# A two-layer decoder trunk on one core: the SBUF layout turned round, overlaid regions lowest

## The chip, the cores and the metric

One Trainium2 chip, one of its cores. The metric is the device time of one execution in microseconds. The median of three runs of the kernel before is 2397.23 us (2395.22 to 2398.16).

## The reference

Two layers over 512 tokens of width 1024, everything float32:

```python
for l in range(DEPTH):
    h = h + 0.5 * swiglu(rmsnorm(h, ffn1_norm[l]), ffn1_w_in[l], ffn1_w_out[l])
    u = rmsnorm(h, mix_norm[l])
    q_a, c_kv, iq, ik, iw, z_pool, q_c, gate_pre = jnp.split(u @ w_in[l], split_pts, axis=-1)
    y_a = dsa_attention(q_a, c_kv, iq, ik, iw, w_uk[l], w_uv[l], rel_bias)   # top-128 of the causal keys
    y_b = pool_mixer(z_pool, w_pool[l], pool_scale[l])
    y_c = mem_attention(q_c, rmsnorm(mem, mem_norm[l]), w_mem_kv[l])
    g = jax.nn.sigmoid(gate_pre).reshape(B, S, N_BRANCH, D)
    merged = (g[:, :, 0] * (y_a @ w_branch_a[l]) + g[:, :, 1] * (y_b @ w_branch_b[l])
              + g[:, :, 2] * (y_c @ w_branch_c[l]))
    h = h + merged @ w_out[l]
    h = h + 0.5 * swiglu(rmsnorm(h, ffn2_norm[l]), ffn2_w_in[l], ffn2_w_out[l])
return rmsnorm(h, final_norm)
```

A SwiGLU block has a hidden width of 2816.

## The kernel before, in words

The activations lie transposed, features on the 128 partitions and the 512 tokens in the row, eight tiles of 128 x 512 for a width of 1024. A row of such a tile is 512 floats, 2048 bytes. Every large product is made with split operands: a float32 value is kept as a high part in fp32r and a low part (what the rounding left), and three matmuls of 128x128 by 128x512 stand for one exact tile product: high by high (line 517), low weight by high activation (518), high weight by low activation (519). This is the function `exact`. TensorE loads the 128x128 weight tile and streams the 512 columns of the activation tile past it; the streamed operand is called the moving one here, the loaded one the stationary one.

- **Weights.** SP sends each unit of weights (up to 128 x 1024) from HBM into one of four slots of `raw`. GpSimd (POOL) splits it into `wH` and `wL` (lines 468 and 471), two slots each. TensorE uses a unit, then frees the slot. The order of the units is written out by hand, the same on all engines, and counted by semaphores.
- **FFN** (twice a layer): the hidden tiles come from `u0H`/`u0L` (24 matmuls a unit of 1024 columns), in two halves of 12 and 10 tiles, and go to `hidH`/`hidL`; VectorE (DVE) and ScalarE (ACT) apply norm, sigmoid, gate and split. The down projection streams `hidH`/`hidL` (18 or 15 matmuls a unit).
- **Mixer**: the memory keys and values (lines 605 to 607, 617 to 619, 256 columns; in the first three the normed memory in `yH`/`yL` is the moving operand, in the last three the weights are), the projection `W_in` from `u1H`/`u1L` in slots into which the attention's small matmuls are set by a plan, the gated branches from `yH`/`yL` (a part in the gate slots, `W_branch_a` after them), and `W_out`, again from `u1H`/`u1L`.
- **Start**: in `block.scalar`, lines 851 to 858, a table of T5 biases is written from the tile `q` to HBM (`bias_rows`) and read back spread over the partitions. ACT's first norm step stands behind the first of these two.

**Memory.** `sb(name, shape)` takes the next free piece of each partition's SBUF, in the order of the calls, rounded up to a multiple of 32 bytes; leaving an `ExitStack` gives its pieces back, so that the next stack overlays them. First come the tiles that live through the whole kernel (`h`, `u1H`, `u1L`, `raw`, `wH`, `wL`, tables, scratch), and above them four stacks on one another: `ffn` (`u0H`, `u0L`, `hidH`, `hidL`, `mem`), `mix` (`yH`, `yL`, `gate_a`, `q`, `probs` and others), `index` and `late`. `exact` is:

```python
for i, (t, k) in enumerate(tiles):
    a, b = wH[:, w, t * P:(t + 1) * P], wL[:, w, t * P:(t + 1) * P]
    pe.matmul(dst, a, hi[:, k, :], start=first and i == 0, stop=False)
    pe.matmul(dst, b, hi[:, k, :], start=False, stop=False)
    mm = pe.matmul(dst, a, lo[:, k, :], start=False, stop=last and i == len(tiles) - 1)
```

Of the kernel before, what the change touches and what calls it, by code (L numbers as in the profile page):

```python
# [22 lines left out]
F32R = mybir.dt.float32r  # L23
# [4 lines left out]
P = 128  # L28
D = 1024
T = 512  # L30
L = 2
M = 256
KD = D // P
QB = T // P
H = 8
HD = 64
R = 128
IH = 8
# [14 lines left out]
RAW_SLOTS, SPLIT_SLOTS, BANKS = 4, 2, 4  # L53
# [15 lines left out]
W_POOL, W_UK, W_UV, N_PAR = 35, 163, 675, 1187  # L69

K_ID, K_ONE, K_CAUSAL, K_COUNT, K_GAIN, N_CONST = 0, 128, 256, 384, 416, 424

N_SCORES = 3 * IH
NBIAS = 384


def attention_steps():
# [91 lines left out]
def bucket_of(n):  # L169

    exact = BUCKETS // 2
    nf = np.maximum(n, 1).astype(np.float32)
    large = exact + (np.log(nf / np.float32(exact)) / np.float32(math.log(MAXDIST / exact))
                     * np.float32(BUCKETS - exact)).astype(np.int32)
    return np.where(n < exact, n, np.minimum(large, BUCKETS - 1))


def constants():
# [6 lines left out]
    for g, w in enumerate(WINDOWS):  # L185
        rows = slice(64 * (g % 2), 64 * (g % 2) + 64)
        first = 1.0 / np.minimum(np.arange(1, WMAX + 1), w)
        c[rows, K_COUNT + WMAX * (g // 2):K_COUNT + WMAX * (g // 2) + WMAX] = first
    buckets = bucket_of(np.maximum(255 - np.arange(NBIAS), 0))
    hot = (np.arange(BUCKETS)[:, None] == buckets[None, :]).astype(np.float32)  # L190
# [3 lines left out]
def trunk(nc, xT, memT, wA, wB0, wB1, wM, wR, par, const, hot, rel, out, bias_rows):  # L194
    ctx = ExitStack()
    with ctx:
        def sb(name, shape, dt=F32, scope=ctx):
            return scope.enter_context(nc.sbuf_tensor(name, shape, dt))
# [2 lines left out]
            return ctx.enter_context(nc.semaphore(name))  # L201


        h = sb("h", [P, KD, T])
        u1H, u1L = sb("u1H", [P, KD, T], F32R), sb("u1L", [P, KD, T], F32R)
        raw = sb("raw", [P, RAW_SLOTS, 8 * P])
        wH = sb("wH", [P, SPLIT_SLOTS, 8 * P], F32R)
        wL = sb("wL", [P, SPLIT_SLOTS, 8 * P], F32R)
        near_bias = sb("near_bias", [P, H, 2 * P])
        far_bias = sb("far_bias", [P, H])  # L210
        cst = sb("cst", [P, N_CONST])
        pr = sb("pr", [P, N_PAR])
        rms = sb("rms", [P, T])
        mem_rms = sb("mem_rms", [P, M])
        ssq = sb("ssq", [P, T])
        sq = sb("sq", [P, T])
        ta = sb("ta", [P, T])
        tb = sb("tb", [P, T])
        sg = sb("sg", [P, 2, T])
        iw = sb("iw", [P, QB, IH])  # L220
        norm = sb("norm", [P, 3, QB])
        top8 = sb("top8", [P, 8])
        nmax = sb("nmax", [P, 4, 2])
        rsum = sb("rsum", [P, 4, 2])
        rinv = sb("rinv", [P, 4, 2])

        with ExitStack() as ffn:
            u0H, u0L = sb("u0H", [P, KD, T], F32R, ffn), sb("u0L", [P, KD, T], F32R, ffn)
            hidH = sb("hidH", [P, HALF[0], T], F32R, ffn)
# [29 lines left out]
        with ExitStack() as late:  # L259
            sb("hole0", [P, 2, KD, T], F32, late)  # L260
            sb("hole1", [P, KD, T], F32, late)
            part = sb("part", [P, KD, T], F32, late)
            gate_bc = sb("gate_bc", [P, 2, T], F32, late)
        mem_hi = yH[:, 0:4, :].rearrange("p a (b m) -> p (a b) m", m=M)
        mem_lo = yL[:, 0:4, :].rearrange("p a (b m) -> p (a b) m", m=M)
        c_tok = ssq[:, :].rearrange("p (b r) -> p b r", r=R)
# [11 lines left out]
        rel_sb = q[0:BUCKETS, 1, 0:H]  # L278
        bias_table = q[0:H, 2, 0:NBIAS]

# [125 lines left out]
        def _(sp):  # L406
            sp.dma_start(cst[:, :], const).then_inc(const_loaded, 16)

            sp.dma_start(q[0:BUCKETS, 0, 0:NBIAS], hot).then_inc(rel_loaded, 16)
            sp.dma_start(q[0:BUCKETS, 1, 0:H], rel).then_inc(rel_loaded, 16)  # L410
# [86 lines left out]
        def _(pe):  # L497
# [34 lines left out]
            def spread(diag, n, cols=T):  # L532
# [6 lines left out]
            pe.wait_ge(rel_loaded, 32)  # L539
            pe.matmul(sbank[0][0:H, 0:NBIAS], rel_sb, q[0:BUCKETS, 0, 0:NBIAS], start=True, stop=True  # L540
                      ).then_inc(bias_full, 1)
# [284 lines left out]
        def _(act):  # L826
# [13 lines left out]
            for k in range(KD):  # L840
# [4 lines left out]
                if k:  # L845
# [4 lines left out]
            act.wait_ge(bias_full, 1)  # L850
            act.activation(bias_table, sbank[0][0:H, 0:NBIAS], ACT.Copy).then_inc(bias_copied, 1)
            act.wait_ge(bias_copied, 1)

            act.dma_start(bias_rows, bass.AP(tensor=bias_table.tensor, offset=bias_table.offset,
                                             ap=[bias_table.ap[0], [0, P], [1, NBIAS]])).then_inc(bias_stored, 16)
            act.wait_ge(bias_stored, 16)
# [666 lines left out]
```

## Time and profile before

| | before |
|---|---|
| median of three runs | 2397.23 us |
| the profiled execution, its own time | 2396.16 us |
| its span, first to last instruction | 2394.3 us |
| TensorE matmul (PE) busy | 2312.5 us, 97% |
| GpSimd (POOL) busy | 1389.6 us, 58% |
| VectorE (DVE) busy | 1249.8 us, 52% |
| ScalarE (ACT) busy | 560.3 us, 23% |
| granted TensorE clock, mean | 0.989 |

The profile is of one execution. Its span leaves out 1.9 us that the time of the same execution holds. The durations of matmuls overlap, since they are pipelined and their ends are modelled: what one costs is read from the distance between two starts.

### The profile page before, as it was taken

What the parts mean: (1) busy time and instruction counts of PE and PEld (TensorE: products, weight loads), DVE (VectorE), ACT (ScalarE), POOL (GpSimd) and SP (SyncE); (2) the same over time, 40 slices, a digit from 0 to 9 for tenths busy, and PEclk for the clock granted to TensorE, in tenths of its full rate; (3) what the DMA queues carried; (4) which work ended last, traced back from release to release, by engine and by line L of the source; (5) the groups of instructions that cost most, each with busy time, mean ns of one, the idle gap of its engine ahead of it and who ended that gap; (6) DMA issues with size and microseconds to landing.
All of it is one profiled execution on the core that took longest, in us unless ns stands there. A gap on an engine that the chain in (4) does not pass through costs nothing.

```text
span 2394.3 us, 31804 instructions
## 1 busy us (share of the span) xinstructions
PE 2312.5 (97%) x10328; PEld 1846.1 (77%) x10328; DVE 1249.8 (52%) x1756; ACT 560.3 (23%) x1038; POOL 1389.6 (58%) x868
## 2 busy tenths in 40 slices
PE   3999999999999999999999999999999999999997
PEld 2788888777877788888778888877777778888875
DVE  2453355478865755225454524636787566440453
ACT  1211112243455221001121101214334532110111
POOL 2566666634434666666666666664344366666663
PEclk8999999999999999999999999999999999999998
DMA  5233223311121322232232332232121122223222
GB/s 136 90 116 95 97 87 98 101 58 66 58 67 49 112 91 89 88 104 85 81 107 96 110 103 91 80 110 80 54 64 61 53 97 89 97 79 105 96 76 73
DMA packets 66482, 208.74 MB, mean 87 GB/s; under 512 B 7352, under 2 KB 9560, under 8 KB 66136
## 3 DMA queue, kind: packets, MB, share of 16 engines
q1 hardware_dynamic: 63600, 202.84, 25.7%
q10 hardware_dynamic: 2792, 4.72, 0.9%
q8 instruction: 54, 0.88, 0.2%
q14 instruction: 36, 0.29, 0.0%
HBM read 203.86 MB, written 3.67 MB: 87 GB/s over the span
## 4 chain that ended last, share of the span: by engine, by line
PE 89%; DVE 7%; DMA 2%; issue 1%; ACT 1%; DVEq 0%; ACTq 0%
PE bank L517 27%; PE bank L519 27%; PE bank L518 27%; DMA bias_rows<-q 1%; PE obank L737 1%; PE sbank L689 1%; PE tbank L710 1%; DVE u1L L1429 1%; DVE picks L1229 1%; DVE picks L1252 1%; DVE tb L1443 1%; PE sbank L684 1%; PE obank L724 1%; DVE top L1227 1%; PE sbank L671 1%
## 5 line engine op out<-in xcount | busy, mean ns | idle before, releaser
L468 POOL TENSOR_SCALAR wH<-raw 128x1024 fp32r<-128x1024 f32 (+3 forms) x432 | 438.2, 1014 | 944.6 <-PE bank L519 926.8
L471 POOL TENSOR_TENSOR wL<-raw,wH 128x1024 fp32r<-128x1024 f32 (+3 forms) x432 | 951.5, 2202 | 36.0
L517 PE MATMUL bank<-u0H,wH 128*128 128x512 f32 x1408 | 563.3, 400 | 6.9 <-POOL wL L471 4.1
L518 PE MATMUL bank<-u0H,wL 128*128 128x512 f32 x1408 | 559.7, 398 | 0.0
L519 PE MATMUL bank<-u0L,wH 128*128 128x512 f32 x1408 | 559.7, 397 | 0.0
L517 PEld LDWEIGHTS bank<-u0H,wH 128*128 128x128 f32 x1408 | 266.1, 189 | 76.5 <-issue 8.5
L518 PEld LDWEIGHTS bank<-u0H,wL 128*128 128x128 f32 x1408 | 266.4, 189 | 65.3 <-issue 1.2
L519 PEld LDWEIGHTS bank<-u0L,wH 128*128 128x128 f32 x1408 | 266.2, 189 | 65.0
L517 PE MATMUL bank<-u1H,wH 128*128 128x512 f32 x704 | 295.7, 420 | 7.5 <-DVE u1L L1429 3.1
L517 PE MATMUL bank<-hidH,wH 128*128 128x512 f32 x704 | 279.6, 397 | 0.7 <-DVE hidL L1132 0.7
L518 PE MATMUL bank<-hidH,wL 128*128 128x512 f32 x704 | 279.1, 396 | 0.0
L519 PE MATMUL bank<-hidL,wH 128*128 128x512 f32 x704 | 279.0, 396 | 0.0
L519 PE MATMUL bank<-u1L,wH 128*128 128x512 f32 x704 | 275.9, 392 | 0.0
L518 PE MATMUL bank<-u1H,wL 128*128 128x512 f32 x704 | 274.9, 391 | 0.0
L1123 DVE TENSOR_TENSOR tb<-bank,rms 128x512 f32<-128x512 f32 x88 | 60.8, 691 | 356.4 <-PE bank L519 356.4
L1129 DVE TENSOR_TENSOR sg<-ta,tb 128x512 f32<-128x512 f32 x88 | 232.4, 2641 | 3.0
L869 ACT ACTIVATE hidH<-sg 128x512 f32 x88 | 55.6, 632 | 698.6 <-DVE sg L1129 698.6
L517 PEld LDWEIGHTS bank<-u1H,wH 128*128 128x128 f32 x704 | 132.3, 188 | 51.9 <-issue 20.0
L517 PEld LDWEIGHTS bank<-hidH,wH 128*128 128x128 f32 x704 | 132.6, 188 | 33.8 <-DVE hidL L1132 1.5
L519 PEld LDWEIGHTS bank<-hidL,wH 128*128 128x128 f32 x704 | 132.6, 188 | 32.3
L518 PEld LDWEIGHTS bank<-hidH,wL 128*128 128x128 f32 x704 | 132.6, 188 | 32.2
L519 PEld LDWEIGHTS bank<-u1L,wH 128*128 128x128 f32 x704 | 132.1, 188 | 29.6
(175 smaller groups left out, 2411.0 us busy)
## 6 DMA issues: line engine op xcount, KB each, us to landing
raw<-in_wA SPq DMA_DIRECT2D x176, 512.0 KB, 3.3
raw<-in_wM SPq DMA_DIRECT2D x96, 512.0 KB, 3.3
raw<-in_wB SPq DMA_DIRECT2D x64, 384.0 KB, 3.0
raw<-in_wB SPq DMA_DIRECT2D x64, 320.0 KB, 2.9
raw<-in_wR SPq DMA_DIRECT2D x32, 256.0 KB, 2.6
h<-in_xT ACTq DMA_DIRECT2D x4, 512.0 KB, 6.8
mem<-in_memT SPq DMA_DIRECT2D x2, 1024.0 KB, 6.8
outT<-gate_a SPq DMA_DIRECT2D x4, 512.0 KB, 2.7
```

What stands on the lines that cost most here:

```text
L468: pool.tensor_scalar(wH[:, w, 0:cols], raw[:, slot, 0:cols], 1.0, 0.0, ALU.mult, ALU.add).then_inc(rounded, 1)
L471: pool.tensor_tensor(wL[:, w, 0:cols], raw[:, slot, 0:cols], wH[:, w, 0:cols].bitcast(F32), ALU.subtract).then_inc(split_done, 1)
L517: pe.matmul(dst, a, hi[:, k, :], start=first and i == 0, stop=False)
L518: pe.matmul(dst, b, hi[:, k, :], start=False, stop=False)
L519: mm = pe.matmul(dst, a, lo[:, k, :], start=False, stop=last and i == len(tiles) - 1)
L671: mm = pe.matmul(dst[:, j * M:(j + 1) * M], qc[rows, j, a * P:(a + 1) * P], kc[rows, j, :], start=True, stop=True)
L684: mm = pe.matmul(dst[:, j * P:(j + 1) * P], pr[rows, W_UK + P * j:W_UK + P * (j + 1)], q[rows, j, a * P:(a + 1) * P], start=True, stop=True)
L689: mm = pe.matmul(dst[:, 0:width], qlat[:, b, :], ckv[:, 0:width], start=True, stop=True)
L710: mm = pe.transpose(tbank[:, kb * P:(kb + 1) * P], probs[:, m % 3, kb * P:(kb + 1) * P], ident)
L869: act.activation(hidH[:, bass.ds(j * 2 + i, 1), :].rearrange("p a t -> p (a t)"), sg[:, 1, :], ACT.Copy).then_inc(hidden_high, 1)
L1123: dve.tensor_tensor(tb[:, :], bank[2 * i + 1][:, :], rms[:, :], ALU.mult).then_inc(evacuated, 1)
L1129: dve.tensor_tensor(sg[:, 1, :], ta[:, :], tb[:, :], ALU.mult).then_inc(gated, 1)
```

## The change

The four overlaid stacks are opened first, from the lowest free address on, and after them one piece `overlays` of 24,704 floats (98,816 bytes) takes their place for good, so that the tiles of the whole kernel come above. Nothing else is changed: every engine has the same instructions on the same tiles in the same order, three lines further down in the file.

```diff
+OVERLAYS = 24704
...
+        with ExitStack() as ffn:
+            u0H, u0L = sb("u0H", [P, KD, T], F32R, ffn), sb("u0L", [P, KD, T], F32R, ffn)
+            hidH = sb("hidH", [P, HALF[0], T], F32R, ffn)
+            hidL = sb("hidL", [P, HALF[0], T], F32R, ffn)
+            mem = sb("mem", [P, KD, M], F32, ffn)
+        with ExitStack() as mix:
+            yH, yL = sb("yH", [P, KD, T], F32R, mix), sb("yL", [P, KD, T], F32R, mix)
...
+        with ExitStack() as late:
...
+            gate_bc = sb("gate_bc", [P, 2, T], F32, late)
+        sb("overlays", [P, OVERLAYS])
 
         h = sb("h", [P, KD, T])
         u1H, u1L = sb("u1H", [P, KD, T], F32R), sb("u1L", [P, KD, T], F32R)
...
         rinv = sb("rinv", [P, 4, 2])
-
-        with ExitStack() as ffn:
-            u0H, u0L = sb("u0H", [P, KD, T], F32R, ffn), sb("u0L", [P, KD, T], F32R, ffn)
...
```

The start of each tile in a partition, in bytes, as the built programs have it. All overlaid tiles move down by 112,288 and all others up by 98,816:

| tile | start before | mod 64 | start after | mod 64 |
|---|---|---|---|---|
| h | 16,512 | 0 | 115,328 | 0 |
| u1H, u1L | 32,896; 49,280 | 0 | 131,712; 148,096 | 0 |
| raw (4 slots) | 65,664 | 0 | 164,480 | 0 |
| wH, wL | 82,048; 90,240 | 0 | 180,864; 189,056 | 0 |
| near_bias | 98,432 | 0 | 197,248 | 0 |
| cst | 106,656 | 32 | 205,472 | 32 |
| pr | 108,352 | 0 | 207,168 | 0 |
| rms, ssq, sq, ta, tb, sg | 113,120 to 124,384 | 32 | 211,936 to 223,200 | 32 |
| u0H, yH | 128,800 | 32 | 16,512 | 0 |
| u0L, yL | 145,184 | 32 | 32,896 | 0 |
| hidH, gate_a | 161,568 | 32 | 49,280 | 0 |
| hidL | 186,144 | 32 | 73,856 | 0 |
| q | 198,432 | 32 | 86,144 | 0 |
| mem, probs | 210,720 | 32 | 98,432 | 0 |

A tile's rows of 512 floats follow one another at steps of 2048 bytes, so each has the remainder of its tile.

## Rows read from the trace of the kernel before

**Rows 1.** The page: span, TensorE's share, its granted clock, and the chain by engine.
```profile
span 2394.3 us, 31804 instructions
...
PE 2312.5 (97%) x10328; PEld 1846.1 (77%) x10328; DVE 1249.8 (52%) x1756; ACT 560.3 (23%) x1038; POOL 1389.6 (58%) x868
...
PEclk8999999999999999999999999999999999999998
...
PE 89%; DVE 7%; DMA 2%; issue 1%; ACT 1%; DVEq 0%; ACTq 0%
```
**Rows 2.** Timeline of PE, last W_out unit into FFN: start, length (us), line, tiles.
```profile
831.97 0.39 PE L517 MATMUL bank<-u1H,wH 128*128 128x512 f32 x1
...
837.41 0.40 PE L517 MATMUL bank<-u0H,wH 128*128 128x512 f32 x1
...
838.11 0.39 PE L517 MATMUL bank<-u0H,wH 128*128 128x512 f32 x1
...
842.80 0.40 PE L519 MATMUL bank<-u0L,wH 128*128 128x512 f32 x1
```
**Rows 3.** Timeline of PE, among the gate slots of layer 0.
```profile
683.17 0.39 PE L517 MATMUL bank<-u1H,wH 128*128 128x512 f32 x1
...
684.98 0.39 PE L519 MATMUL bank<-u1L,wH 128*128 128x512 f32 x1
...
700.28 0.39 PE L518 MATMUL bank<-yH,wL 128*128 128x512 f32 x1
...
702.61 0.39 PE L519 MATMUL bank<-yL,wH 128*128 128x512 f32 x1
```
**Rows 4.** Line 518 by tile: count, ns min/median/max, first and last start, forms.
```profile
L518 PE MATMUL bank<-u0H,wL x1408: 392/397/628, 13.7 to 2317.5; 128*128 128x512 f32 x176
L518 PEld LDWEIGHTS bank<-hidH,wL x704: 187/188/192, 186.8 to 2374.1; 128*128 128x128 f32 x176
L518 PE MATMUL bank<-hidH,wL x704: 392/397/400, 187.1 to 2374.4; 128*128 128x512 f32 x176
...
L518 PE MATMUL bank<-u1H,wL x704: 387/389/402, 443.3 to 2000.9; 128*128 128x512 f32 x176
...
L518 PE MATMUL bank<-yH,wL x128: 388/394/400, 616.5 to 1953.7; 128*128 128x512 f32 x128
```
**Rows 5.** Timeline of PE, the 256-column products of the memory projection.
```profile
424.80 0.28 PE L607 MATMUL bank<-yL,wH 128*128 128x256 f32 x1
...
427.26 0.28 PE L607 MATMUL bank<-yL,wH 128*128 128x256 f32 x1
...
439.32 0.28 PE L619 MATMUL bank<-wH,yL 128*128 128x256 f32 x1
...
441.83 0.28 PE L619 MATMUL bank<-wH,yL 128*128 128x256 f32 x1
```
**Rows 6.** Stretches: length, busy us and counts by engine, PEclk, DMA share, GB/s.
```profile
0.00:59.00 59.00, 21.23 (x70) 13.98 (x70) 17.32 (x18) 11.71 (x18) 14.94 (x12) 0.83 0.54 138
...
764.00:792.00 28.00, 26.64 (x112) 20.56 (x111) 22.16 (x23) 11.23 (x18) 21.52 (x19) 1.00 0.35 113
```
**Rows 7.** Timeline of ACT at the start: the store and load of the biases.
```profile
24.39 1.28 ACTq L854 DMA_DIRECT2D bias_rows<-q  x1
59.21 0.39 ACTq L858 DMA_DIRECT2D near_bias<-bias_rows  x1
```
**Rows 8.** Waits of PE: us in total, times, longest.
```profile
PE obank L535 <- DVE tb L1086: 31.6, 2, 29.1
```
**Rows 9.** Groups by form, PE: a short attention product (busy us, mean ns).
```profile
L684 PE MATMUL sbank<-q,pr 64*128 64x128 f32 x128 | 18.5, 285 | 0.0
```
**Rows 10.** Groups by form, POOL: splitting a 640-column unit (busy us, mean ns).
```profile
L471 POOL TENSOR_TENSOR wL<-raw,wH 128x640 fp32r<-128x640 f32 x64 | 103.2, 1612 | 5.3
...
L468 POOL TENSOR_SCALAR wH<-raw 128x640 fp32r<-128x640 f32 x64 | 48.8, 763 | 80.7 <-PE bank L519 80.7
```

More of the change, by code:

```diff
@@ L201, in sem @@
             return ctx.enter_context(nc.semaphore(name))
[L204 to L225, printed above, removed]
         with ExitStack() as ffn:
@@ L263, in trunk @@
             gate_bc = sb("gate_bc", [P, 2, T], F32, late)
+        sb("overlays", [P, OVERLAYS])
+        h = sb("h", [P, KD, T])
+        u1H, u1L = sb("u1H", [P, KD, T], F32R), sb("u1L", [P, KD, T], F32R)
+        raw = sb("raw", [P, RAW_SLOTS, 8 * P])
+        wH = sb("wH", [P, SPLIT_SLOTS, 8 * P], F32R)
+        wL = sb("wL", [P, SPLIT_SLOTS, 8 * P], F32R)
+        near_bias = sb("near_bias", [P, H, 2 * P])
+        far_bias = sb("far_bias", [P, H])
+        cst = sb("cst", [P, N_CONST])
+        pr = sb("pr", [P, N_PAR])
+        rms = sb("rms", [P, T])
+        mem_rms = sb("mem_rms", [P, M])
+        ssq = sb("ssq", [P, T])
+        sq = sb("sq", [P, T])
+        ta = sb("ta", [P, T])
+        tb = sb("tb", [P, T])
+        sg = sb("sg", [P, 2, T])
+        iw = sb("iw", [P, QB, IH])
+        norm = sb("norm", [P, 3, QB])
+        top8 = sb("top8", [P, 8])
+        nmax = sb("nmax", [P, 4, 2])
+        rsum = sb("rsum", [P, 4, 2])
+        rinv = sb("rinv", [P, 4, 2])
         mem_hi = yH[:, 0:4, :].rearrange("p a (b m) -> p (a b) m", m=M)
```

## The prediction

> **What bounds the kernel now.** The page comes first: TensorE has a matmul in flight for 97% of the 2394.3 us, its clock is granted in full in nearly every slice, and the chain that ends last is 89% TensorE [rows 1]. So the time is the number of matmuls times the distance between their starts, and I read distances. The change adds, removes and reorders no instruction; it can act only through addresses. The question for the trace is therefore whether a matmul's price depends on where its operands lie, and for that I compared like products on different tiles.
>
> The border between `W_out` and the second FFN is the cleanest place [rows 2]. From 831.97 to 837.41 TensorE starts 24 matmuls that stream `u1H`/`u1L`: 5.44 us, **226.7 ns each**. From 837.41 to 842.80 it starts 23 more that stream `u0H`/`u0L`: 5.39 us, **234.3 ns each**. Shape, types, weight buffers and clock are the same and nothing lies between. The reader is to see a step at the moment when the moving tile changes. In the gate slots it happens inside one stage, in both directions [rows 3]: 8 steps on `u1` take 1.81 us (226 ns), 10 steps on `y` 2.33 us (233 ns). And it holds everywhere: over all uses the median modelled length is 397 ns for `u0`, 397 for `hid`, 394 for `y` and 389 for `u1`, with minima of 392, 392, 388 and 387 [rows 4].
>
> What do the dear tiles have in common? In the table of starts, `u0`, `hid` and `y` begin 32 bytes past a multiple of 64, `u1` on one; the stationary `wH`/`wL` are on one for all. It isn't merely that the dear ones lie above 131,072 bytes: the first tile of `u0H` spans 128,800 to 130,848, and its three matmuls (the third streams `u0L`) take 838.11 - 837.41 = 0.70 us, 233 ns each, like the rest [rows 2]. As an estimate from the rows: were a 2048-byte row read in pieces of 64 bytes, a start on a multiple would need 32 pieces and a start 32 off 33, and 226.7 x 33/32 = 233.8, beside 234.3 measured. One row speaks against so simple a picture: among the 256-column products, 21 steps with `y` moving take 2.46 us (117.1 ns) and 21 with the weights moving and `y` stationary 2.51 us (119.5 ns) [rows 5]. There one operand is 32 off in both forms, so they say nothing of two aligned operands, but they show no toll on the moving side alone. After the change every moving tile of line 517 to 519 and every weight tile is on a multiple of 64, which is the state of `u1` today.
>
> **The change part by part.**
>
> *FFN products.* 1408 on each of three lines for `u0` and 704 on each for `hid`, as line 518 shows [rows 4]: 3 x 2112 = 6336. At the start some are covered: up to 59 us 70 matmuls have run, 10 of them for biases and norm, so 60 of the FFN [rows 6], and then TensorE waits up to 29.1 us for the norm's `tb` [rows 8], which waits for ACT behind the bias store. These 60 save nothing. The toll: 234.3 - 226.7 = 7.6 at the border [rows 2], 233 - 226 = 7 in the gate slots [rows 3]; I take 7.1 ns, between the two and equal to 1/33 of 234.3. 6276 x 7.1 = **44.6 us**. Bounds are the differences of medians [rows 4]: `y` less `u1`, 5 ns, gives 31.4; `u0` less `u1`, 8 ns, gives 50.2. Does TensorE stay the bound? The tightest feeder is the 640-column unit: 15 matmuls fall from 3.51 to 3.41 us, and POOL needs 0.763 + 1.612 = 2.38 us for its split [rows 10]. It keeps 1 us.
>
> *Branch products on `y`.* 3 x 128 = 384. Half of them stand in the gate slots, where TensorE is the chain: 192 x 7.1 = **1.4 us**. The other half are `W_branch_a`, where DVE is busy 22.2 of 28 us with the merging and TensorE 26.6 [rows 6]; what they save is waited for at the first merged tile of `W_out`. I cost this half at 0, with 1.4 us as the upper bound; the cover is DVE's chain, and without it the 1.4 us come too.
>
> *Small products of the attention* (128 on `q` [rows 9], as many on `ckv`, fewer on `kc` and `ik_stack`) stream short rows, some 370 in all. At most 7.1 ns each, 2.6 us; at least 0, since their neighbours' waits may take it. I take **1.0 us**. The 256-column products I cost at 0.
>
> *`u1` products* (2112) keep their remainder and their weights' remainder: 0. *DVE, ACT, POOL:* `raw`, `wH`, `wL`, `rms`, `ta`, `tb`, `sg` all move by the same 98,816 bytes, a multiple of 64: 0, under TensorE's cover.
>
> *The bias store.* From issue at 24.39 to the next instruction at 59.21, 34.8 us pass [rows 7], and nearly all of it is on the path. It reads eight partitions of `q`, which move from 32 to 128 bytes past a multiple of 256. I know no row that prices this; I take 0, with -1 and +2 us as bounds. The Trainium skill (DMA: Bandwidth & Descriptors, How a descriptor splits into AXI transactions) has a transaction begin on a multiple of 256 bytes: an estimate by it is 49 beats for a packet before and 52 after, 6% more, or about 2 us longer; with it the sum would be 2 us worse. No run here shows it yet.
>
> *What comes back.* Between the hidden products and the down projection the last gate and split of DVE take as long as before while TensorE arrives sooner, so some of these eight borders lose a little: **-0.5 us**.
>
> Sum: 44.6 + 1.4 + 1.0 - 0.5 = 46.5 us. The profiled execution took 2396.16 us, 1.07 under the median of 2397.23; taken from that median, 2350.7 us. **Forecast 2350.5 us**, 1.95% faster. Within its own case it lies between 2343 (8 ns, and something from `y` and the short products: 2350.7 - 5.6 - 2) and 2366 (5 ns: 2350.7 + 13.2, and the DMA 2 longer).
>
> **The rivals.**
>
> *B: no difference, 2397 us.* The step belongs to something other than the start: what DVE and ACT do beside, or which tile they are writing. For it: FFN, `hid` and `y` differ from `u1` in more than address, and the 256-column rows show no toll [rows 5]. Against: inside one stage the price goes up for `y` and back for `u1` [rows 3], at full clock and with the same neighbours. The Trainium skill (SBUF — State Buffer, Specifications) gives 16-byte cachelines with a penalty for each new line; both remainders are multiples of 16, so by that rule a row crosses equally many lines and the change is worth nothing. Chance 10%.
>
> *C: height, not remainder, 2365 us.* The toll begins somewhere between 65,664 (the end of `u1L`) and 128,800. Then `u0`, `hid`, `y` come free, 46.5 us, and `u1`, now from 131,712 on, pays: 2112 x 7.1 = 15.0. 2397.2 - 46.5 + 15.0 = 2365.7. If `hidL` above 73,856 kept its toll, 704 x 7.1 = 5 more. For it: the trace can't exclude it. Against: no threshold lies at a natural place, 131,072 being excluded by the first tile of `u0H`. Chance 6%.
>
> *D: slower.* TensorE reads two streams at once, weights and moving columns. Before, no moving tile above 131,072 bytes ever met weights that lay there too, since `wH`/`wL` were at 82,048 to 98,432. Afterwards the 2112 products on `u1` do. Should the two reads get in each other's way in one half, the products of `W_in` and `W_out` grow. A load takes 188 ns [rows 4], hidden under the stream; bounds are 0 and 188 ns a product. The point from which the kernel gets slower is 46.5 us / 2112 = 22 ns. At a quarter of a load, 47 ns, it is 2350.7 + 99 = 2450 us. Against: no tile shows such a toll in the present layout. Chance 3%.
>
> **How the numbers follow.** Forecast 80%, B 10%, C 6%, D 3%, and 1% for what I don't see. The forecast's own range holds some 95% of its case, 0.76, and half of C lies inside it, 0.03: together about 0.80, so the range is 2343 to 2366. A measurement of this kernel can tell about 0.2% (4.8 us) from no change. Faster is the forecast and C, 0.86; same is B, 0.10; slower is D and half of the rest, 0.04.
>
> **What would show it.** In the profile afterwards the step at the border from `u1` to `u0` is gone and both go at 227 ns; line 518 has a median of 389 ns for all four tiles; POOL waits some 45 us less for TensorE, while the busy time of DVE, ACT and POOL stays. C would show `u0` at 227 and `u1` at 234; B the same step as now; D a `u1` distance above 250 ns. The forecast is wrong if `u0` isn't below 230 ns, or if it is and the time falls by less than 35 us: then a wait has taken the gain, and I would look at the bias store and at `W_out`'s first tiles.

## The result and the profile after

The changed kernel takes **2346.84 us** (median of four runs, 2344.18 to 2348.62), the kernel before 2397.55 us in the four runs beside and before it. The ratio is 0.9787, with a 95% interval of 0.9775 to 0.9799: 2.1% faster, 50.7 us. The forecast was 2350.5 in a range of 2343 to 2366. The profiled execution took 2346.86 us with a span of 2345.0 (before: 2396.16 and 2394.3).

The page after, in the lines that answer to [rows 1]:

```profile
span 2345.0 us, 31804 instructions
...
PE 2263.2 (97%) x10328; PEld 1839.8 (78%) x10328; DVE 1250.0 (53%) x1756; ACT 560.1 (24%) x1038; POOL 1406.7 (60%) x868
...
PEclk8999999999999999999999999999999999999998
...
PE 87%; DVE 8%; DMA 2%; ACT 1%; issue 1%; DVEq 0%; POOL 0%; ACTq 0%; POOLq 0%
```

The instruction counts are the same to the last one, DVE and ACT are busy as long as before (1250.0 and 560.1 us against 1249.8 and 560.3), and the span and the busy time of TensorE have both fallen by 49 us. POOL is busy for 17.1 us more (1406.7 against 1389.6), which the prediction didn't expect. It is the border between `W_out` and the second FFN that shows where the gain came from, as in [rows 2] (timeline of PE: start, length in us):

```profile
821.62 0.39 PE L520 MATMUL bank<-u1H,wH 128*128 128x512 f32 x1
...
827.06 0.39 PE L520 MATMUL bank<-u0H,wH 128*128 128x512 f32 x1
...
832.27 0.39 PE L522 MATMUL bank<-u0L,wH 128*128 128x512 f32 x1
```

24 starts from 821.62 to 827.06 are 226.7 ns apart, as before; the 23 that follow, on `u0`, take 5.21 us, 226.5 ns. The step of 7.6 ns is gone. Line 518 is line 521 now, and its median lengths have come together, where [rows 4] had 397, 397 and 394 beside 389 (count, ns min/median/max):

```profile
L521 PE MATMUL bank<-u0H,wL x1408: 387/389/628, 14.4 to 2270.3; 128*128 128x512 f32 x176
...
L521 PE MATMUL bank<-hidH,wL x704: 387/389/397, 182.7 to 2325.4; 128*128 128x512 f32 x176
...
L521 PE MATMUL bank<-yH,wL x128: 387/389/402, 606.7 to 1916.5; 128*128 128x512 f32 x128
```

By stage, from stretches of the two traces that begin and end with the same instructions (length, then busy us and counts of PE, PEld, DVE, ACT, POOL). Before: the first down projection, then the mixer of layer 0 without `W_out`, then the first hidden half of the second FFN:

```profile
186.80:254.60 67.80, 67.80 (x293) 54.55 (x291) 16.84 (x20) 5.15 (x10) 44.42 (x32) 1.00 0.31 98
...
443.00:791.70 348.70, 342.73 (x1667) 269.73 (x1667) 242.02 (x473) 152.42 (x330) 159.77 (x105) 1.00 0.20 67
...
837.40:974.10 136.70, 136.70 (x587) 109.76 (x586) 71.11 (x70) 25.00 (x33) 89.14 (x48) 1.00 0.26 90
```

The same after:

```profile
182.50:248.20 65.70, 65.70 (x294) 54.45 (x292) 16.50 (x21) 5.15 (x10) 44.39 (x33) 1.00 0.33 103
...
433.20:781.30 348.10, 341.98 (x1666) 269.65 (x1666) 241.66 (x474) 152.33 (x330) 159.94 (x105) 1.00 0.21 67
...
827.10:959.50 132.40, 132.40 (x588) 109.41 (x587) 71.00 (x70) 24.98 (x33) 90.81 (x48) 1.00 0.28 92
```

The FFN stretches lose 3.1% of their length, the mixer 0.6 us of 348.7. Read from the exact first start of each stage, the FFN stretches (with the start, the memory projection and the tail) differ by 47.8 us in all, the two mixers with `W_out` by 1.5.

The memory projection is one stage where the two traces differ for another reason. Its two uses before, then its two uses after:

```profile
424.50:443.00 18.50, 15.33 (x107) 14.34 (x107) 8.48 (x18) 2.73 (x4) 14.35 (x9) 0.91 0.35 113
1586.80:1607.00 20.20, 16.98 (x107) 16.00 (x107) 8.36 (x18) 2.74 (x4) 14.48 (x9) 0.83 0.32 104
```

```profile
413.10:433.20 20.10, 17.05 (x107) 15.96 (x107) 8.30 (x18) 2.73 (x4) 14.41 (x9) 0.83 0.32 104
1553.60:1570.70 17.10, 14.03 (x106) 13.00 (x106) 8.56 (x18) 2.73 (x4) 14.41 (x9) 1.00 0.36 123
```

The column before the DMA share is TensorE's granted clock. Where it is below 1, a part of these products starts at 213 ns distances in place of 112 to 120: that part ran at the lower of the clock's two levels (1.2 in place of 2.4 GHz), after a pause of TensorE that leads up to it (busy 1.22 of 3.00 us from 415 to 418 us in the trace after). The first use became 1.6 us longer and the second 3.0 us shorter. In the eleven kernels of this document each use takes about 17.1, 18.5 or 20.1 us, and the toll doesn't order them: the four kernels with the FFN at 226.7 ns have 20.1 and 17.1 three times and 18.6 and 18.6 once. So these 1.4 us net are not the step that was forecast, and whether the change brought them isn't shown.

### The profile page after: what moved, and what is told of

Read it like the earlier page. It is cut to its first block, busy times and chain, and to the rows that moved or that the text cites. A ratio compares the mean times of both kernels' runs of the same rounds, so it can differ in the third digit from the quotient of the medians.

```text
span 2345.0 us, 31804 instructions
## 1 busy us (share of the span) xinstructions
PE 2263.2 (97%) x10328; PEld 1839.8 (78%) x10328; DVE 1250.0 (53%) x1756; ACT 560.1 (24%) x1038; POOL 1406.7 (60%) x868
## 4 chain that ended last, share of the span: by engine, by line
PE 87%; DVE 8%; DMA 2%; ACT 1%; issue 1%; DVEq 0%; POOL 0%; ACTq 0%; POOLq 0%
PE bank L520 27%; PE bank L522 26%; PE bank L521 26%; PE obank L740 1%; DMA bias_rows<-q 1%; PE sbank L692 1%; PE tbank L713 1%; DVE u1L L1432 1%; DVE tb L1446 1%; DVE picks L1232 1%; DVE picks L1255 1%; PE sbank L687 1%; PE obank L727 1%; DVE top L1230 1%; PE sbank L674 1%
## 5 line engine op out<-in xcount | busy, mean ns | idle before, releaser
L471 POOL TENSOR_SCALAR wH<-raw 128x1024 fp32r<-128x1024 f32 (+3 forms) x432 | 454.6, 1052 | 878.7 <-PE bank L522 862.0
L520 PE MATMUL bank<-u0H,wH 128*128 128x512 f32 x1408 | 553.2, 393 | 7.7 <-POOL wL L474 4.5
L522 PE MATMUL bank<-u0L,wH 128*128 128x512 f32 x1408 | 549.6, 390 | 0.0
L521 PE MATMUL bank<-u0H,wL 128*128 128x512 f32 x1408 | 549.4, 390 | 0.0
L522 PE MATMUL bank<-hidL,wH 128*128 128x512 f32 x704 | 274.0, 389 | 0.0
L521 PE MATMUL bank<-hidH,wL 128*128 128x512 f32 x704 | 273.9, 389 | 0.0
L1132 DVE TENSOR_TENSOR sg<-ta,tb 128x512 f32<-128x512 f32 x88 | 232.2, 2638 | 3.0
L521 PEld LDWEIGHTS bank<-u1H,wL 128*128 128x128 f32 x704 | 132.6, 188 | 28.2 <-issue 3.4
```

The source lines that it names most:

```text
L471: pool.tensor_scalar(wH[:, w, 0:cols], raw[:, slot, 0:cols], 1.0, 0.0, ALU.mult, ALU.add).then_inc(rounded, 1)
L1132: dve.tensor_tensor(sg[:, 1, :], ta[:, :], tb[:, :], ALU.mult).then_inc(gated, 1)
```

## The experiments

The twelve runs (numbered 1 to 12) either move tiles and do nothing else, or measure the products by themselves. "48 starts" counts the distances from the first row shown to the second. "d" is the start of the moving tile less the start of its weight buffer, modulo 256 bytes; it is 160 for `u0`, `hid` and `y` in the kernel before, 0 in the changed one, and 0 for `u1` in both. This quantity wasn't in the prediction; it came out of the first four runs.

**1. 32 bytes ahead of the overlaid tiles, in the kernel before.**

```diff
+        sb("pad", [P, 8])
         with ExitStack() as ffn:
```

> The kernel before with 32 bytes put between the whole kernel's tiles and the overlaid ones: u0, hid and y stay high (from 128,832) but now begin on a multiple of 64. Theory R (the remainder of the moving tile by 64 sets the price, 227 or 234 ns): all four tiles at 227 ns, 2347 us, the same as the changed kernel. Theory H (height: tiles high in SBUF are dear): u0 and hid stay at 234 ns, 2397 us. Theory M (mismatch: dear when the remainders of moving and stationary tile differ): as R, 2347 us.

Measured: 2389.48 us, ratio to before 0.9973 (0.9963 to 0.9983). The moving tiles lay on multiples of 64, and yet 48 starts on `u0` took 11.20 us, 233.3 ns each (timeline of PE):

```profile
859.82 0.39 PE L518 MATMUL bank<-u0H,wH 128*128 128x512 f32 x1
...
871.02 0.39 PE L518 MATMUL bank<-u0H,wH 128*128 128x512 f32 x1
```

Theory R, the one of my prediction, fell here: on a multiple of 64 the product still costs 6.6 ns too much. Theory M as it is written, with remainders by 64, fell with it, since both operands were on multiples of 64; it can live on only with a longer period.

**2. The changed kernel with its overlaid tiles 32 bytes higher.**

```diff
+        sb("pad", [P, 8])
         with ExitStack() as ffn:
...
-        sb("overlays", [P, OVERLAYS])
+        sb("overlays", [P, OVERLAYS + 8])
```

> The changed kernel with every overlaid tile 32 bytes higher and all others 64 bytes higher: u0, hid and y lie low but 32 past a multiple of 64; u1 and the weights stay on multiples. R and M: u0, hid, y at 234 ns, u1 at 227, 2397 us (2394 to 2399). H: all at 227 ns, 2347 us.

Measured: 2390.29 us, 0.9975 of before (0.9963 to 0.9986). 48 starts take 11.20 us, 233.3 ns:

```profile
859.71 0.40 PE L521 MATMUL bank<-u0H,wH 128*128 128x512 f32 x1
...
870.91 0.40 PE L521 MATMUL bank<-u0H,wH 128*128 128x512 f32 x1
```

Lying low is worth nothing: theory H fell. All but about 6 us of the change can be lost by shifting the low tiles by 32 bytes. The time is 4 us under the range expected by R and M, since the toll was 6.6 ns here and 7.6 before.

**3. Everything 32 bytes higher.** As run 2, with `OVERLAYS` left as it is.

> The changed kernel with every tile 32 bytes higher, so that moving and stationary tiles are all 32 past a multiple of 64. R: every product pays, u1 too: 234 ns throughout and 2397 + 2112 x 7.1 = 2412 us. M: the remainders agree, 227 ns throughout, 2347 us. H: 2347 us.

Measured: 2348.9 us, 0.9804 of before (0.9789 to 0.9818), with every tile of line 517 to 519 and every weight tile 32 past a multiple of 64. 48 starts take 10.88 us, 226.7 ns:

```profile
859.71 0.39 PE L521 MATMUL bank<-u0H,wH 128*128 128x512 f32 x1
...
870.59 0.39 PE L521 MATMUL bank<-u0H,wH 128*128 128x512 f32 x1
```

So no tile's own remainder explains the toll. What the good runs share is the difference between the moving tile and the weights.

**4. The weight buffers alone 32 bytes higher, in the changed kernel.**

```diff
+        sb("pad", [P, 8])
         wH = sb("wH", [P, SPLIT_SLOTS, 8 * P], F32R)
         wL = sb("wL", [P, SPLIT_SLOTS, 8 * P], F32R)
+        sb("pad_after", [P, 8])
```

> The changed kernel with wH and wL alone 32 bytes higher (the tiles behind them 64): moving tiles on multiples of 64, weights 32 past. R and H: 227 ns throughout, 2347 us. M: 234 ns throughout, 2412 us. If a weight load that starts off a multiple costs TensorE something of its own, the load of 188 ns gets longer while the start distance of 227 ns stays.

Measured: 2394.72 us, the same as before (0.9995, 0.9985 to 1.0004). No moving tile was touched, and they all became dear, `u1` with them: 48 starts on `u0` in 11.20 us and 24 on `u1` in 5.60, 233.3 ns each:

```profile
821.93 0.40 PE L522 MATMUL bank<-u1H,wH 128*128 128x512 f32 x1
...
827.53 0.40 PE L522 MATMUL bank<-u1H,wH 128*128 128x512 f32 x1
...
860.07 0.40 PE L522 MATMUL bank<-u0H,wH 128*128 128x512 f32 x1
...
871.27 0.40 PE L522 MATMUL bank<-u0H,wH 128*128 128x512 f32 x1
```

A mismatch between the two operands is what is left, theory M with another period. Run 1 narrows it: there both tiles were on multiples of 64 and the product was still dear, so the period is above 64 bytes. M's own number, 2412 us, was 17 too high. The toll on `u0` and `hid` was 6.6 ns, where its sum keeps the 7.6 of before, and `u1` didn't pay in full: the two mixers with `W_out` take 797.3 us against 787.3 in the changed kernel, 10.0 us for 2112 products on `u1` and 384 on `y`, some 4 ns each. The loads themselves are no longer than before, 188 ns in the median in every kernel.

**5. The four FFN tiles at odd places**, in the changed kernel: each is a view into a tile 16 floats longer, 4, 12, 1 and 2 floats in for `u0H`, `u0L`, `hidH`, `hidL`.

```diff
+            def off(name, n, words):
+                whole = sb(name, [P, n * T + 16], F32R, ffn)
+                return whole[:, words:words + n * T].rearrange("p (a t) -> p a t", t=T)
```

> The changed kernel with the four FFN tiles at other remainders by 64: u0H 16, u0L 48, hidH 4, hidL 8 bytes; u1 and y stay at 0. Theory R in pieces of 64 bytes (a row that starts anywhere inside a piece touches 33 of them): 234 ns for all three products of u0 and of hid, as with 32, and 2394 to 2399 us. Theory S (16-byte lines: only a start inside a line costs): u0 at 227, hid at 234 or above, 2347 + 2112 x 7.1 = 2362 us. A toll that grows with the remainder would set u0L (48) above u0H (16) and hid lowest.

Measured: 2407.35 us in one run, 9 us above the before of that hour (2398.14). d is 16 and 112 for `u0H` and `u0L`, 132 and 200 for `hidH` and `hidL`. On `u0` 48 starts take 11.31 us (235.6 ns), on `hid` 11.52 us (240.0 ns):

```profile
859.92 0.40 PE L523 MATMUL bank<-u0H,wH 128*128 128x512 f32 x1
...
871.23 0.40 PE L523 MATMUL bank<-u0H,wH 128*128 128x512 f32 x1
...
1009.60 0.41 PE L523 MATMUL bank<-hidH,wH 128*128 128x512 f32 x1
...
1021.12 0.41 PE L523 MATMUL bank<-hidH,wH 128*128 128x512 f32 x1
```

Both theories fell, R with 234 ns for all four tiles and S with 227 ns for `u0`. It is no matter of yes or no: the price is graded, and the layout before wasn't the worst.

**6. The products by themselves.** A program in which nothing but TensorE runs after the loading.

> A program by itself: 192 products to warm up, then blocks of 96 products each, with nothing running beside on any other engine: streamed tile 0, 32, 16, 48 or 4 bytes past a multiple of 64 with weights on a multiple, then 0 and 32 with weights 32 past; rows of 512, 384 and 256 columns. It computes none of the reference. R with one piece more for a row: 7 ns more for every start off 0, at each of the three lengths, unless the 188 ns load limits. A rate theory (each piece of a row off a multiple costs a little): 7 ns at 512 columns, 5 at 384, 3.5 at 256. If the toll comes only from other engines' traffic: no difference between blocks.

The blocks don't divide by the moving tile's remainder, and the 7 ns that R wanted for every start off 0, at each length, isn't there: the order of the prices is another at each length. The tiles' starts made d 192, 160, 80, 240, 4, 96 and 64 in the order of the blocks; d = 0 wasn't among them. For example, d = 4 and then d = 96 and 64 (line by tile: count, ns min/median/max, first and last start):

```profile
L55 PE MATMUL bank<-mfour,wzero x96: 390/399/406, 149.3 to 171.8; 128*128 128x512 f32 x96
L55 PE MATMUL bank<-mzero,whalf x96: 391/394/400, 172.0 to 194.2; 128*128 128x512 f32 x96
L55 PE MATMUL bank<-mhalf,whalf x96: 387/392/397, 194.4 to 216.2; 128*128 128x512 f32 x96
```

With 95 steps in each they go, by the exact starts, at 236.5, 233.3 and 229.0 ns. d = 160 (82.21 to 104.47 us) gave 234.3 ns, exactly what the kernel before shows at 160. Two things follow: the toll needs no other engine, since none runs; and it is set by the two operands of TensorE itself.

**7. The remaining tiles on multiples of 64**, a pad of 8 floats behind each tile whose length leaves the next one 32 past.

> The changed kernel with the remaining tiles that begin 32 past a multiple (cst, rms, mem_rms, ssq, sq, ta, tb, sg and the small ones) moved onto multiples of 64 by pads. R: only the attention's short products on sg and cst and the nine norm products on tb and ssq could gain; their start distance is about 110 ns, set by something other than the stream, so 2347 us within 2 us. If ACT, DVE or POOL had a toll too, their durations on ta, tb, sg would fall (DVE 691 ns, ACT 633 ns) but not the time by more than 3 us.

Measured: 2346.58 us, 0.9782 of before (0.9769 to 0.9796), no different from the changed kernel; DVE's and ACT's durations stand. `u0` goes at 226.7 ns (10.88 us for 48 starts). Scratch and tables needn't be touched.

**8. The kernel before with 96 bytes in place of 32.** d becomes 0, and the overlays stay on top.

```diff
+        sb("pad", [P, 24])
         with ExitStack() as ffn:
```

> The kernel before with 96 bytes, in place of 32, put between the whole kernel's tiles and the overlaid ones. u0, hid and y stay high (from 128,896). Counted from the weight buffers, the moving tiles now begin a multiple of 128 bytes away, as u1 does in every fast run so far. Theory D (the distance between moving tile and weight tile, by a multiple of 128, sets the price): all four tiles at 227 ns and 2347 us, like the changed kernel, with the overlays still on top. Theory R (moving tile alone, by 64) has fallen; a height theory gives 2397 us; a theory of 512 (u0 is now 256 past one) gives 233 ns and 2390 us.

Measured: **2346.81 us**, 0.9791 of before (0.9778 to 0.9805). 48 starts take 10.88 us, 226.7 ns:

```profile
859.75 0.39 PE L520 MATMUL bank<-u0L,wH 128*128 128x512 f32 x1
...
870.63 0.39 PE L520 MATMUL bank<-u0L,wH 128*128 128x512 f32 x1
```

That is the whole of the change's gain from one pad of 96 bytes, without turning anything round. It also limits the period: `u0` was 256 past a multiple of 512 from the weights, so the period divides 256. Theory D with 128 bytes says the same here; runs 9 and 12 tell them apart.

**9. The price by distance**, products by themselves.

> A program by itself, computing none of the reference: 96 products a block, streamed tile a multiple of 512 bytes from the weights plus 0, 4, 8, 16, 48 and then 32, 64 up to 480 bytes, rows of 512, then 384, then 256 columns. Theory D128: at 512 columns 227 ns at plus 0, 128, 256 and 384, and 229 to 237 ns elsewhere. D256: 227 at 0 and 256 alone. D512: at 0 alone. The two earlier points taken over: plus 192 at 233.3, plus 32 at 234. If any distance gives less than 227 ns, there is a better layout than the changed one. At 256 columns, 117 to 123 ns with another pattern, since the load of the next weights takes another place in the stream.

Blocks of 96 products, 95 steps, at 512 columns (the tile's name tells its distance from the weights beyond a multiple of 512):

```profile
L54 PE MATMUL bank<-plus000b,w x96: 389/389/389, 44.8 to 66.4; 128*128 128x512 f32 x96
L54 PE MATMUL bank<-plus004b,w x96: 395/398/401, 66.6 to 89.1; 128*128 128x512 f32 x96
...
L54 PE MATMUL bank<-plus064b,w x96: 387/392/394, 178.4 to 200.2; 128*128 128x512 f32 x96
...
L54 PE MATMUL bank<-plus128b,w x96: 392/394/398, 222.8 to 245.0; 128*128 128x512 f32 x96
...
L54 PE MATMUL bank<-plus160b,w x96: 388/397/400, 245.2 to 267.5; 128*128 128x512 f32 x96
...
L54 PE MATMUL bank<-plus256b,w x96: 389/389/395, 312.5 to 334.0; 128*128 128x512 f32 x96
...
L54 PE MATMUL bank<-plus384b,w x96: 392/395/398, 401.0 to 423.2; 128*128 128x512 f32 x96
```

From the exact starts the distances are 226.7 ns at 0, 236.6 at 4, 233.3 at 32, 228.9 at 64, 233.4 at 128, 234.2 at 160, 233.2 at 192 and 224, 226.7 at 256, 229.0 at 320, 233.4 at 384. From 256 on the list repeats to within 0.2 ns at the eight places 0 to 224 in steps of 32: at 512 columns **the period is 256 bytes**, D128 and D512 fell. At other lengths the list is another one. At 256 columns (busy us, mean ns) d = 0 is among the dear places and 64 and 192 are cheap in this program:

```profile
L54 PE MATMUL bank<-plus000b,w 128*128 128x256 f32 x96 | 11.7, 283 | 0.0
...
L54 PE MATMUL bank<-plus192b,w 128*128 128x256 f32 x96 | 11.1, 276 | 0.0
L54 PE MATMUL bank<-plus064b,w 128*128 128x256 f32 x96 | 11.0, 276 | 0.0
```

By starts these are 119.8, 113.7 and 113.4 ns; at 384 columns everything lies between 173.3 and 176.6. At 256 columns the difference modulo 256 doesn't settle the price: 320 gave 117.8 ns where 64 gave 113.4, and run 6 had 117.8 at both 64 and 192. At 384 columns run 6 reached 179.9, at d = 240.

**10. The same in steps of 4 bytes.**

> A program by itself, computing none of the reference: 64 blocks of 72 products, 512 columns, streamed tile a multiple of 512 bytes from the weights plus 0, 4, 8 up to 252 bytes. Theory D256 with the changed kernel at the best place: 226.7 ns at plus 0 and no lower value anywhere. Rival: some distance between the multiples of 16 tried so far is cheaper, which would give a layout better than the changed one (each ns is 8.8 us of the kernel, 8832 products of 512 columns). Points taken over: 0, 4, 8, 16, 32, 48, 64 at 226.7, 236.6, 233.2, 231.7, 233.3, 230.0, 228.9.

Blocks of 72 products, 71 steps:

```profile
L54 PE MATMUL bank<-plus000b,w x72: 389/389/390, 67.1 to 83.1; 128*128 128x512 f32 x72
...
L54 PE MATMUL bank<-plus020b,w x72: 399/404/405, 150.4 to 167.4; 128*128 128x512 f32 x72
...
L54 PE MATMUL bank<-plus028b,w x72: 387/387/391, 184.4 to 200.5; 128*128 128x512 f32 x72
...
L54 PE MATMUL bank<-plus240b,w x72: 388/388/389, 1073.5 to 1089.6; 128*128 128x512 f32 x72
```

The 64 places run from 226.7 to 239.9 ns; 226.7 or 226.9 is reached at 0, 28, 60, 156, 236, 240 and 252, and nowhere is it less. So within this family of layouts the changed kernel's 512-column products are at the floor. Two places came out unlike in two programs (48: 230.0 and 233.2; 240: 233.3 in run 6, 226.7 here), with the same d: it doesn't settle everything. What else does is open.

**11 and 12. Two middle places in the kernel**: pads of 160 and of 224 bytes in the kernel before, d = 64 and 128 (`[P, 40]` and `[P, 56]` in the diff of run 8).

> The kernel before with 160 bytes between the whole kernel's tiles and the overlaid ones: u0, hid and y begin 64 bytes past a multiple of 256 from the weights. Theory D256 with the micro program's price list: 229 ns, between the two states so far, and 2347 + 6276 x 2.2 = 2361 us. A yes-or-no theory of 64 bytes (on a multiple: 227): 2347 us. A yes-or-no theory of 128: 233 to 234 ns, 2390 us.

> The same with 224 bytes: u0, hid and y begin 128 bytes past a multiple of 256 from the weights. D256: 233.4 ns and 2347 + 6276 x 6.7 = 2389 us. D128 (any multiple of 128 is cheap): 227 ns and 2347 us.

Measured: 2362.86 us, 0.9853 of before (0.9837 to 0.9869), and 2382.14 us, 0.9937 (0.9921 to 0.9954). 48 starts take 10.99 us (229.0 ns) with the pad of 160:

```profile
859.83 0.39 PE L520 MATMUL bank<-u0L,wH 128*128 128x512 f32 x1
...
870.82 0.39 PE L520 MATMUL bank<-u0L,wH 128*128 128x512 f32 x1
```

and 11.16 us (232.5 ns) with the pad of 224:

```profile
860.02 0.39 PE L520 MATMUL bank<-u0L,wH 128*128 128x512 f32 x1
...
871.18 0.40 PE L520 MATMUL bank<-u0L,wH 128*128 128x512 f32 x1
```

The price list of run 9 carries over to the kernel within 0.1 ns at 64 and within 0.9 ns at 128 (233.4 there), where the 2389 us expected are 7 too many. Both yes-or-no theories fell, and so did D128. Put together, with 226.7 ns as the floor and 6276 products on `u0` and `hid`:

| kernel | d | start distance, ns | 2346.8 + 6276 x excess, us | measured, us |
|---|---|---|---|---|
| before, pad 96 | 0 | 226.7 | 2346.8 | 2346.8 |
| changed, all 32 up | 0 | 226.7 | 2346.8 | 2348.9 |
| before, pad 160 | 64 | 229.0 | 2361.2 | 2362.9 |
| before, pad 224 | 128 | 232.5 | 2383.2 | 2382.1 |
| before, pad 32 | 192 | 233.3 | 2388.2 | 2389.5 |
| changed, overlays 32 up | 224 | 233.3 | 2388.2 | 2390.3 |
| before | 160 | 234.3 | 2394.5 | 2397.6 |

The sum misses the measured times by -1.1 to 3.1 us. Of that the bias store accounts for 0, 0.9 or 1.7 us, by its own list below: 1.7 in "before", "all 32 up" and "overlays 32 up", 0.9 with the pads of 32 and 160, 0 with those of 96 and 224. What is then left is -1.1 to 1.4 us, for `y`, the short products, the memory projection's clock and the scatter of the medians; it isn't divided further. Two kernels aren't in the table. With the odd places of run 5, means of 235.4 ns on `u0` and 238.3 on `hid` over the whole trace give 2346.8 + 36.2 + 24.5 = 2407.5 us, and 2407.35 were measured. With the weights moved (run 4), 41.4 for the FFN and the 10.0 us of the mixers give 2398.2 us: the profiled execution took 2397.8, but the median of ten is 2394.7, so this one is 3.5 us too high.

## Why the prediction was right, and where its reason was wrong

**The bound and the place** were right. The time is the number of matmuls times the distance of their starts; those on `u0`, `hid` and `y` changed to the distance of `u1`; nothing took more than some 2 us of the gain on the way. What would prove the forecast wrong (`u0` not below 230 ns, or less than 35 us) didn't come. Of the other signs, the medians of line 518 are all 389 ns, as said; POOL waits 65 us less for TensorE, not 45, and its busy time didn't stay.

**The step that failed** is "What do the dear tiles have in common?". I read from the table of starts that the moving tile's own remainder by 64 decided, and even had an estimate that agreed, 226.7 x 33/32 = 233.8. Runs 1, 3 and 4 each break it: 233.3 ns on a multiple of 64, 226.7 ns 32 off one, 233.3 ns after moving only the weights. What decides is the distance between moving tile and weight tile, with a period of 256 bytes. In the two layouts the prediction compared, both rules say the same, because `wH` and `wL` stood on a multiple of 64 in both and `u0` happened to fall 128 bytes into 256 like them; the rows of one kernel that I used could not tell them apart. So it was luck that the reason I had gave the right place for the tiles: a layout turned round with another sum of sizes could have put them on multiples of 64 and won only some 6 us, as run 1 did. The estimate 226.7 x 33/32 agreed by luck too. The 256-column rows [rows 5] were the warning: they showed no toll on the moving side alone, and I named them and went on. Run 9 shows that such products have another price list, and the rows fit it: `y` moving had d = 160 (117.1 ns there, 117.4 in run 9), the weights moving had 96 (119.5 and 120.0).

**The terms.**

- *FFN products*, forecast 44.6 us: the toll was 234.3 - 226.8 = 7.5 ns (means of all start distances under 260 ns, before and after), not 7.1, so 47.1 us; the start distances themselves, added up, fell by 47.2. The measured step of 7.6 ns at the border was the better reading; I had leaned on the gate slots and on the 1/33 of a wrong picture. These 0.4 ns on 6276 products are most of what the sum, 46.5 us, was short of.
- *`y` and short products*, forecast 1.4 and 1.0: the two mixers together with `W_out` are only 1.5 us shorter (0.6 and 1.0 for the mixers, 0 for `W_out`). Of these `W_branch_a`, costed at 0 for its cover by DVE, gave 0.7 (0.2 and 0.5), so the cover was not whole; the gate slots and the short products gave 0.9 of the 2.4 that I had for them. Why so little is open.
- *The memory projection*, forecast 0: 1.4 us shorter in all, and that is the granted clock of the rows above. The layout made a part of it dearer: its 256-column products with `y` moving went from 117.4 to 117.8 ns to 119.3 to 119.4 at full clock, as run 9's list has it for 160 and 0.
- *The bias store*, forecast 0 with -1 and +2: from issue to the next instruction 33.1 us in place of 34.8 [rows 7]:

```profile
25.13 1.28 ACTq L857 DMA_DIRECT2D bias_rows<-q  x1
58.27 0.39 ACTq L861 DMA_DIRECT2D near_bias<-bias_rows  x1
```

  It is 1.7 us shorter and began 0.7 later. PE's wait for the norm behind it fell by 1.4 (29.5 to 28.0 us between the two starts). The source's remainder by 128 goes with it in all eleven kernels: 33.1 to 33.2 us at 0 (six kernels), 34.0 at 64 (pads of 32 and 160), 34.8 at 32 (before, overlays 32 up, all 32 up). The Trainium skill (DMA: Bandwidth & Descriptors, How a descriptor splits into AXI transactions) gave an estimate of 6% more for this step, since 128 past a multiple of 256 makes a longer tail than 32 past one. The trace shows 5% less for the whole store, and no difference between a source 0 past a multiple of 256 (pad of 224, 33.1 us) and one 128 past (the changed kernel, 33.1), where the rule has 48 and 52 beats. So the rule doesn't price this store; the time of the read alone isn't shown.
- *What comes back*, forecast -0.5 at the borders of the hidden products: 0.1 there (TensorE's waits for `hidL` are 0.8 us against 0.7). But the FFN stages as a whole, with the bias store's 1.4, lost 0.5 us outside the plain steps, so 1.9 came back elsewhere: 0.4 at the first weight unit, 0.5 in three products at the lower clock level after the first norm (starts 427 ns apart, where before they were at 333, 232 and 237), the rest in small pieces.
- *Feeders:* POOL kept up, and waits less for TensorE: 862 us against 927 before its first split operation. TensorE's waits for its weights at line 517 (now 520) grew from 6.8 to 7.9 us. The first split of a 1024-column unit takes 1196 ns in place of 1153, which makes 11.7 of the 17.1 us that POOL is busier. All four kernels at 226.7 ns have it (1405.8 to 1407.0 us busy), the one at 229.0 has most of it (1404.4), those at 232.5 ns and more little or none (1386.1 to 1394.4); what lengthens it is open.

The sum of what was measured is 47.2 (steps of the FFN) - 0.5 (the rest of the FFN stages, the bias store in it) + 1.5 (mixers) + 1.4 (memory projection, by the clock) - 0.4 (the first product comes later) = 49.2 us; the spans of the two profiled executions differ by 49.3. The medians differ by 50.7; the 1.4 between them is within the scatter of the executions.

**The rivals.** B, no difference, is excluded by the result and by the programs of runs 6, 9 and 10, in which nothing runs beside. C, height, is excluded by runs 2 and 8: low tiles can be dear and high ones cheap. D spoke of TensorE's two reads getting in each other's way, by the half of SBUF they lie in. The halves play no part (`u1` above 131,072 bytes with the weights there too goes at 226.7), but that the two reads concern each other was right, and it came nearer to the cause than my forecast's reason.

That the toll comes from the reading of the moving columns meeting the loading of the next weights is an inference: what the runs show is that the two operands' addresses decide together, that no other engine is needed, and that the length of the row changes the list. No run took the loads away. The Trainium skill (SBUF — State Buffer, Who interferes with whom) lists two independent read ports for TensorE, one for the moving operand and one for weight loads; taken by that alone, their relative address would change nothing, while runs 4 and 10 show 6.6 and up to 13 ns a product. The Trainium skill's 16-byte cachelines (SBUF — State Buffer, Specifications) would have put both layouts at the same time, and would not tell d = 32 from d = 0, which are 233.3 and 226.7 ns apart from start to start in run 9.

## What to carry to other kernels

Where TensorE is the bound and streams 512 columns of fp32r per weight load, as here, put the moving tiles a multiple of 256 bytes from the weight tiles: here that was worth 2.1%, and a pad of 96 bytes did it. At 256 columns that is no rule: 0 was among the dear places. The effect is found by comparing the distance of starts between like products on different tiles of one trace, and a layout change "for order" has to be read as a change of all these distances. One trace in which two explanations coincide doesn't choose between them; a run that moves the other operand does, and costs one line.

## What the runs showed of the hardware that I hadn't expected

- The start distance of a 128x128 by 128x512 fp32r product with its weight load runs from 226.7 to 239.9 ns with the relative address of the two operands, in steps as fine as 4 bytes, and repeats after 256 bytes where that was tried (multiples of 32). A shift of both by 32 bytes leaves it. Two places, 48 and 240, gave two values in two programs, so something else has a part. At 256 columns the best places are others (113.4 ns at 64, 119.8 at 0 in run 9), and the second value of 64 there, 117.8 in run 6, shows the other part again.
- The load itself has a median of 188 ns in every kernel, dear or cheap. In run 10 it is 187 to 189 ns at 58 of the 64 places and 190 to 193 at six; the four at 192 or 193 (20, 132, 196, 212) are among the dearest, 238.6 to 239.9 ns from start to start.
- A DMA that reads 1024 times 1536 bytes from eight partitions took 33.1, 34.0 or 34.8 us with its source 0, 64 or 32 bytes past a multiple of 128.
- ACT's and DVE's instructions on `ta`, `tb`, `sg` took as long with these on multiples of 64 (run 7) as 32 off (the changed kernel): 633 and 632 ns for `sg` from `ta` on ACT, 2635 and 2638 for the product of `ta` and `tb` on DVE, 691 and 691 for `tb`.
- TensorE's granted clock fell to its lower level in part of the memory projection in some of the eleven traces' uses of it and not in others: 17.1 us at 1.00, 20.1 at 0.83.
